# Two-block mixer kernel: loading the residual tiles from the weight loader's queue, and splitting one weight tile after a set of clears

## The reference

```python
# first block, each layer l
h  = rms_norm(x) * (1 + scale) + shift            # from the condition c
p  = h @ w_in[l]                                  # 23 column tiles of 128
y  = concat(conv_branch(p), windowed_attention(p), gated_linear_attention(p))
x  = x + gate * (y @ w_out[l])                    # stage "out1"
# second block, each layer l
p  = rms_norm(x, g1[l]) @ w_in2[l]                # stage "in2"
y  = concat(spatial_gating(p), multiscale_pool(p), retention(p))
x  = x + y @ w_out2[l]                            # stage "out2"
x  = x + conv_ffn(rms_norm(x, g2[l]), w_up2[l], w_down2[l])   # "up", "down"
```

## Time and profile before

| | |
|---|---|
| median of three runs | 3848.76 us (3847.05 to 3853.12) |
| the profiled execution, its own time | 3848.76 us |
| its span, first to last instruction | 3847.1 us |
| TensorE matmul busy | 3603.2 us, 94% of the span |
| VectorE, ScalarE, GpSimd busy | 52%, 24%, 37% |
| mean granted TensorE clock | 0.969 of full speed |

### The profile page before, as it was taken

How to read it: one execution, slowest core, us unless ns; L and a number is a source line. 1 busy time by engine, 2 the same in 40 slices (tenths; PEclk the granted TensorE clock), 3 DMA queues, 4 the chain that set the end, 5 groups by cost and what they waited for, 6 DMA issues and landing times.

```text
span 3847.1 us, 48344 instructions
## 1 busy us (share of the span) xinstructions
PE 3603.2 (94%) x19516; PEld 2890.2 (75%) x19516; DVE 1994.7 (52%) x2593; ACT 938.6 (24%) x1528; POOL 1408.3 (37%) x881
## 2 busy tenths in 40 slices
PE   5999997999999899997999999999998899999998
PEld 3786786877678667875788888877777688888886
DVE  5675816468562664233664445455332474644556
ACT  3113634121454232222211011122222221111111
POOL 2222013544103454333633333346432453333334
PEclk8999998999999899998999999999999899999999
DMA  5510010431000342112311111123111321111113
GB/s 201 203 50 12 2 41 19 126 121 34 11 19 23 104 138 66 33 34 67 108 44 47 58 45 41 58 71 115 55 33 33 93 88 50 39 50 55 50 38 94
DMA packets 83948, 247.05 MB, mean 64 GB/s; under 512 B 8720, under 2 KB 11792, under 8 KB 82960
## 3 DMA queue, kind: packets, MB, share of 16 engines
q1 hardware_dynamic: 70320, 214.62, 17.3%
q10 hardware_dynamic: 13408, 29.36, 2.4%
HBM read 227.17 MB, written 16.78 MB: 63 GB/s over the span
## 4 chain that ended last, share of the span: by engine, by line
PE 82%; DVE 13%; ACT 2%; issue 1%; DMA 1%; POOL 0%; SPq 0%; DVEq 0%; ACTq 0%; POOLq 0%
PE banks L663 22%; PE banks L661 22%; PE banks L662 22%; DVE wk L1888 3%; PE banks L777 2%; PE banks L791 2%; PE banks L810 2%; DVE nt L1793 1%; DVE h_lo L1809 1%; PE banks L633 1%; DVE nt L1782 1%; PE banks L1041 1%; PE banks L635 1%; PE banks L634 1%; DVE wk L2044 1%
## 5 line engine op out<-in xcount | busy, mean ns | idle before, releaser
L661 PE MATMUL banks<-h_hi,w_hi 128*128 128x512 f32 (+1 forms) x3504 | 1360.6, 388 | 6.0 <-POOLq L2362 6.0
L663 PE MATMUL banks<-h_hi,w_lo 128*128 128x512 f32 (+1 forms) x3504 | 1344.1, 384 | 0.0
L662 PE MATMUL banks<-h_lo,w_hi 128*128 128x512 f32 (+1 forms) x3504 | 1338.9, 382 | 0.0
L2360 POOL CAST w_hi<-raw 128x1024 fp32r<-128x1024 f32 (+2 forms) x386 | 403.7, 1046 | 2162.9 <-PE banks L663 1884.6
L2361 POOL TENSOR_TENSOR w_lo<-raw,w_hi 128x1024 fp32r<-128x1024 f32 (+2 forms) x386 | 853.0, 2210 | 30.9
L661 PEld LDWEIGHTS banks<-h_hi,w_hi 128*128 128x128 f32 x3504 | 660.4, 188 | 144.1 <-issue 8.8
L662 PEld LDWEIGHTS banks<-h_lo,w_hi 128*128 128x128 f32 x3504 | 659.8, 188 | 142.3 <-issue 8.5
L663 PEld LDWEIGHTS banks<-h_hi,w_lo 128*128 128x128 f32 x3504 | 659.6, 188 | 133.3
L2310 DVE TENSOR_SCALAR nt<-wk,v 128x1024 f32<-128x1024 f32 x88 | 87.1, 990 | 391.8 <-ACTq L1725 373.8
L661 PE MATMUL banks<-g_hi,w_hi 128*128 128x512 f32 x704 | 277.8, 395 | 8.9 <-DVEq L2299 6.2
L1529 ACT ACTIVATE wk<-banks 128x512 f32<-128x512 f32 x200 | 119.1, 595 | 679.0 <-PE banks L663 657.0
(11 more groups left out here) (238 smaller groups left out, 3804.2 us busy)
## 6 DMA issues: line engine op xcount, KB each, us to landing
raw<-w_in SPq DMA_DIRECT2D x114, 512.0 KB, 3.6
raw<-w_ffn SPq DMA_DIRECT2D x96, 512.0 KB, 3.5
raw<-w_out SPq DMA_DIRECT2D x64, 512.0 KB, 3.6
raw<-w_down SPq DMA_DIRECT2D x96, 256.0 KB, 2.6
x<-w_mod SPq DMA_DIRECT2D x16, 1024.0 KB, 6.3
wk<-residual ACTq DMA_DIRECT2D x42, 256.0 KB, 2.8
gw<-w_mod SPq DMA_DIRECT2D x4, 2048.0 KB, 20.5
residual<-x ACTq DMA_DIRECT2D x4, 2048.0 KB, 8.8
```

Of the source, the lines that this page charges most:

```text
L661: mm(o, wh[:, ws], hi[:, at_, t0:t0 + n], start=kt == 0, stop=False)
L662: mm(o, wh[:, ws], lo[:, at_, t0:t0 + n], start=False, stop=False)
L663: last = mm(o, wl[:, ws], hi[:, at_, t0:t0 + n], start=False, stop=kt == nk - 1)
L2360: link(G.tensor_copy(w_hi[:, sl], raw[:, sl]))
```

## The change

There are two edits.

1. All 16 residual tiles of each of the four out stages are issued by SyncE, each right behind the weight load of the same entry; ScalarE issues none. The wait for addition k - 2 moves with them: SyncE now waits for it before tile k, for k of 2 and more, and the weight load of entry k + 1 stands behind that.
2. GpSimd splits weights only up to `k0` of pass 1 ahead of its two waits and the three memsets. The split of `v0` is then done by the `split_through(in2_index(l, "v0"))` at the head of the loop over head pairs, which was already there and did nothing at j = 0.

```diff
-            def load_old(stage, l, d, src, dst):
-
-                t0, w = OLD[stage, l][0]
-                sp.dma_start(dst[d][:, t0:t0 + w], src[:, d, t0:t0 + w]).then_inc(sem[f"xold_in{d}"], 16)
+            def load_old(stage, l, p, d, src, dst):
+                k = 8 * p + d
+                t0, w = OLD[stage, l][p]
+                if k >= 2:
+                    sp.wait_ge(sem["res_ready"], RES0[stage, l] + k - 1)
+                sp.dma_start(dst[k % 2][:, t0:t0 + w], src[:, d, t0:t0 + w]).then_inc(sem[f"xold_in{k % 2}"], 16)
...
                         load_through(INDEX[("out1", l, d, p)])
-                        if p == 0 and d < 2:
-                            load_old("out1", l, d, scratch[0] if l else xT, xold1)
+                        load_old("out1", l, p, d, scratch[0] if l else xT, xold1)
...
-                        if p == 0 and d < 2:
-                            load_old("out2", l, d, scratch[1 + l], xold2)
+                        load_old("out2", l, p, d, scratch[1 + l], xold2)
...
-            def load_old(stage, l, k, src, dst):
-
-
-                if k < 2 * DT:
-                    t0, w = OLD[stage, l][k // DT]
-                    act.wait_ge(sem["res_ready"], RES0[stage, l] + k - 1)
-                    act.dma_start(dst[k % 2][:, t0:t0 + w], src[:, k % DT, t0:t0 + w]).then_inc(sem[f"xold_in{k % 2}"], 16)
-
...
-                    load_old("out1", l, d + 2, old, xold1)
...
-                    load_old("out1", l, DT + d + 2, old, xold1)
...
-                        load_old("out2", l, DT * p + d + 2, scratch[1 + l], xold2)
...
             for l in layers:
-                split_through(in2_index(l, "v0"))
+                split_through(in2_index(l, "k0", 1))
                 pool.wait_ge(sem["po_mixed"], 2 * (l + 1))
```

More of the change, by code:

```diff
@@ L1492, in _ @@
                 now = x2 if l else x
-                old = scratch[0] if l else xT
                 for d in range(DT):
-                    load_old("out1", l, d + 2, old, xold1)
                     act.wait_ge(sem["res_ready"], RES0["out1", l] + d + 1)
```

## The result

The changed kernel takes 3884.35 us, the median of 4 runs (3879.79 to 3893.42). The kernel before took 3850.94 us beside it on the same chip, also a median of 4 (3847.05 to 3855.17). The ratio is 1.0091, with a 95% interval of 1.0068 to 1.0112: slower. Of 24 executions of the changed kernel on record, 23 took 3875.39 to 3899.59 us, and one, in a slow state with a mean granted clock of 0.649, took 5204.9 us and is left out of every comparison. The forecast was 3888, with a range of 3864 to 3900. The profiled execution has a span of 3888.3 us, 41.2 us above the 3847.1 us of before. This is more than the medians differ by (33.4 us), and part of it isn't the change's, as will be seen.

The account below looks back on a forecast made before the run. TensorE was taken to bound the kernel, with 82% of the chain. Edit 2's 15.7 us plus edit 1's 5.3, 7.9, 0 and 10.2 made 39.1 us on 3848.8, giving 3887.9 us (3888), range 3864 to 3900.

Parts of the forecast that it names:

- Waits of TensorE: TensorE idles for late splits ahead of `v0`, in `out1` and at the ends of `out2`; 5.2 and 6.5 us at `v0`.
- The clock: After every TensorE stall near or above 3 us, a lower granted clock costs 2.0 us more, with 0 as lower bound.
- The split of `v0`: Free in its old place; behind the memsets and rope-table wait it costs 15.7 us over both layers, clock included.
- Start of `out1`, layer 0: Weight 3 now waits for addition 0, so its split is late: stall 3.3 us, with the clock 5.3.
- Layer 1: Start of `out1`, layer 1: weight 3 waits for addition 0, landing taken as 4.8 us; stall 5.9 us, with clock 7.9.
- Pass 1 of `out1`, layer 1: Weight 13, issued during ScalarE's store, stalls TensorE 6.1 us, but slack elsewhere absorbs it: 0, bounds -6 and +4.
- Even turns between the queues: Rival in pass 1 of `out1`, layer 1: queues alternate packets, so loads land sooner; -4 to -6 us, 3883, chance 0.09.
- the row: Pass 1 of `out1`, layer 1: weight 13 priced by the 9.0 us a weight took during the store.
- Ends of `out2`: VectorE falls behind, so weights 14 and 15 come late: stalls 0.2 and 2.9 us, with clock 5.1 each, 10.2 for two.
- ScalarE's 56 issues: In the four out stages ScalarE loses 56 issues of about 0.33 us each; costed at nothing, as a wait covers them.
- The steady part: In the steady state of the out stages the weight's later issue stays hidden, with 1.9 us to spare: no cost.

Follow-up runs that it names:

- q_only: Edit 1 alone, the split of `v0` left where it was, against the kernel before: 3875.97 us, ratio 1.0069.
- s_only: Edit 2 alone, the residual tiles issued as before, against the kernel before: 3857.08 us, ratio 1.0023.
- warm_fit: Changed kernel plus 5 (layer 0) and 7 (layer 1) unused filler matmuls ahead of `v0`: 3880.7 us, ratio 1.0058 against the kernel before.
- s_late: Kernel before with the split of `v0` held until VectorE finished pooling windows and gating products, ahead of the `po_mixed` wait and memsets: 3848.76 us, ratio 0.9983.
- c_after: The changed kernel run again unaltered for a second trace: 3893.5 us, one run.
- q_ahead: Edit 1 alone, with the next entry's weight issued ahead of the residual tile's wait, against the kernel before: 3853.75 us, ratio 0.9999.
- q_ahead2: Edit 1 alone, with weights issued two entries ahead of the residual tile, against the kernel before: 3860.5 us, ratio 1.0008.
- best: Kernel before with edit 1, weights two entries ahead, and the split of `v0` held until `sg_mixed`: 3845.74 us, ratio 0.9977.

## Why the prediction came out

The direction, the time and the range were right, and so were nearly all the places: seven new waits, all released by GpSimd, five of them ahead of the entries that the forecast named. The two at the ends of `out2` came one entry sooner, ahead of entry 14 and not of the last. The sum was right in part by luck: one term was 11 us too large, two others were smaller than forecast, and what filled the gap in the profiled execution was mostly not the change's.

- **Waits of TensorE.** Forecast 5.2 + 6.5 + 3.3 + 5.9 + 6.1 + 3.1 + 3.1 = 33.2 us, with 0.2 + 2.9 for each end of `out2`; measured 26.0. Of edit 2's, 5.2 and 6.5 became 4.60 and 6.07. Both edits' waits are shown by q_only and s_only apart.
- **The clock.** 2.0 us for a stall near or above 3 us: warm_fit measured 1.9 and 2.3 us for those ahead of `v0`. Right. Behind the waits of 3.08, 3.30, 5.47 and 2.69 us the granted clock of the next entry was 0.79, 0.77, 0.70 and 0.78, behind that of 0.78 us it was 1.00.
- **The split of `v0` "cost nothing" in its old place: the step that was wrong.** Edit 2 was forecast at 15.7 us and came to 0.7 + 3.9 = 4.6. What the forecast named was priced well: against s_late, where the split is in nobody's way, the wait and the clock cost 6.8 and 8.3 us, where 7.2 and 8.5 were forecast. The missing term is what the old place cost VectorE, and through its wait TensorE: 6.1 and 4.4 us, shown by s_late. It was to be seen in the trace of before, in the 7.82 us of L2166 and the 4.15 us ahead of L1023; the prediction read TensorE's and GpSimd's rows there and not VectorE's. By the ratio of s_only, edit 2 costs some 9 us (3 to 15): the interval holds the 4.6 us of the lag and ends just under the 15.7 of the forecast.
- **Start of `out1`, layer 0:** 5.3 forecast; 4.9, 8.1 and 5.9 in three traces. Right, with a spread of its own: the wait was 3.08, 5.67 and 4.10 us, as TensorE comes at different times against addition 0. **Layer 1:** 7.9 forecast; 5.2 to 5.8. The wait was 3.30 us (4.15 and 4.10 in c_after and q_only) and not 5.9. Two parts of the term were mis-sized: the landing, 3.6 us where 4.8 had been taken from a busier stretch, and addition 0, which came 5.3 us later than in the kernel before where TensorE's lag was already 7.0 us, so 1.7 us sooner against TensorE than forecast.
- **Pass 1 of `out1`, layer 1:** 0 forecast, 2.9 to 3.5 measured, inside the bounds given. The wait was forecast at 6.1 us and was 5.47. The size is uncertain, since five later traces without edit 1 move there by -3.0 to +1.1 us themselves. The next stage takes back part of it and not all: the lag rose from 12.2 to 19.5 us at entry 15 and fell to 15.5 us at the third entry of the next stage.
- **Even turns between the queues.** Tile 12 no longer stands behind the store: it landed 6.6 us after its issue, where VectorE got it some 10.7 us after the issue in the kernel before (1357.01 to 1367.71). But the weight beside it took 8.2 us (8.7 in q_ahead), near the 9.0 of the earlier trace rows, so the row was the right thing to keep. The estimate of some 4 us less, which the prediction drew from a rule and gave without its working, isn't borne out by the weight. The rule itself fits the trace. The Trainium skill, "DMA: Bandwidth & Descriptors", section "Queues, rings and completion order", says that each transfer engine takes turns between its queues packet by packet. The trace agrees, with 330 packets of one queue and 332 of the other between 1374 and 1378 us. The prediction read the 9.0 us as turns that weren't equal; most of what it has above the 4.0 us of the earlier trace rows is the 4.8 us before the weight's first packet (3.2 us for tile 12 in the changed kernel), where 0.96 us is seen without a store. Why the first packet waits so long beside the store isn't shown.
- **Ends of `out2`:** 10.2 us forecast, 4.5 + 1.1 measured. In layer 0 both late weights are there, but the larger wait fell on entry 14 (2.69 us): its weight was issued at 1873.20, 2.8 us later against the lag than forecast: VectorE's two subtractions just before addition 11 took 4.23 us, where they took 2.13 in the kernel before. In layer 1 the one wait is 0.78 us, ahead of entry 14, and the clock behind it was 1.00, so no clock price. The term had the pace of VectorE in one trace as if it were fixed.
- **ScalarE's 56 issues:** nothing, as forecast; q_ahead2 removes them without the waits and is no faster. The steady part holds as well: from entry 5 to entry 12 of `out1`, layer 1, the lag stays at 12.2 us.

**The total.** The forecast's places hold 24 to 27 us of lag, 12 to 15 less than forecast. The profiled execution reached 41.2 us because it also holds 12.1 us of slow pace and some 6 us ahead of `out1`, layer 1, and behind the up and down stages. The ratio makes 35 us (26 to 43) of it.

Does the slow pace fall into more executions of the changed kernel? The times on record don't say so. Its 23 executions fall into 16 of 3875.4 to 3886.4 us and 7 of 3892.5 to 3899.6. The 29 of the kernel before on the chip of s_late fall into 23 of 3847.5 to 3857.8 and 6 of 3862.1 to 3867.9. The gap between the groups is about the slow pace, and its share is much alike, 7 of 23 and 6 of 29. The medians of the two lower groups, 3881.35 and 3853.3 us, differ by 28 us, though they need not come from one chip. That is close to the 24 to 27 of the named places.

The rest is open. The 3.1 us ahead of `out1`, layer 1, are none of the edits' waits, as said above, but the kernel before has them in neither of its traces. The row behind the up and down stages of layer 0 may be edit 1's: by the starts of GpSimd's casts it is 1.6 to 3.0 us in seven of the eight traces with that edit (q_ahead2 and best among them, -0.3 us in warm_fit) and -0.1 to 0.7 us in the five others. The granted clock doesn't tell them apart: it is 0.83 there in the changed kernel and 0.91 in the kernel before, but 0.82 in s_only. By which way the edit would do it was not found.

## What to carry to other kernels

Work that is hidden on one engine need not be free while it runs beside another engine that is late itself: before costing a moved piece at its new place, price its old place too, from the neighbour's durations with and without it. A wait moved into an in-order queue costs at the edges of a stage, where the consumer lags, and not in its steady middle; issuing the loads behind it two entries ahead took that cost away. Count the clock beside a stall: in these traces it fell behind waits of 2.69 us and more, at some 2 us each where that was measured, and stayed at 1.00 behind one of 0.78 us and behind the 1.82 us of the earlier trace rows.

## What the runs showed of the hardware

VectorE and GpSimd slowed each other here, where both read and wrote 128x1024 tiles of four-byte numbers. VectorE's four additions took 7.82 us with the split beside them and 4.99 without; GpSimd's subtraction took 3.21 us beside them and 2.34 in s_late. Alone, the three pieces make 4.99 + 1.04 + 2.34 = 8.37 us; together they took 7.82, so of the split's 3.38 us only 0.55 overlapped. The Trainium skill, "SBUF — State Buffer", section "SBUF: two separate sides", says that an operation of VectorE with two SBUF inputs and one of GpSimd that reads SBUF take turns on a shared port pair, each blocking the other for a whole instruction. The traces agree in the main: nearly the full length of the cast (0.8 of 1.04 us) and of the subtraction (2.0 of 2.34) was added to VectorE's time.

At a granted clock of 1.00, with TensorE never idle, matmuls of one shape followed each other by 0.228 us on the mean in one execution and by 0.233 in another, through all of an up and down stage, in one layer or the other or in neither. It is in six of the fourteen traces, one layer each, and costs some 12 us every time. Nothing in the profile that I found tells the two apart, and the cause stays open. The twelve times of s_late fall into two groups, 3837.6 to 3844.2 and 3853.3 to 3863.9, which is about this distance.

Two loads beside a large store on another queue were late in good part by their start. With ScalarE's 2 MB store under way, the first packet of SyncE's queue came 3.2 us after the issue in the changed kernel and 4.8 us after it in the kernel before, against 0.96 us for a tile without a store. Between 1374 and 1378 us, in the changed kernel, the two queues moved packets in equal numbers (330 and 332). The weights landed after 8.2 and 9.0 us, where one without a store took 3.6.
